# Twenty-four of the 368 expert-weight loads of a two-layer trunk, each split into three DMAs of 112, 8 and 8 partitions

## The reference

```python
def swiglu(h, w1, w3, w2):
    return (jax.nn.silu(h @ w1) * (h @ w3)) @ w2

def moe_swiglu(h, w_router, w1, w3, w2):
    logits = (xt @ w_router).astype(jnp.float32)
    top_val, top_idx = lax.top_k(logits, TOP_K)          # 2 of 8
    gate = jax.nn.softmax(top_val, axis=-1)
    ...
    for e in range(N_EXPERTS):
        y = y + combine[:, e:e + 1] * swiglu(xt, w1[e], w3[e], w2[e])
```

## Time and profile before

| | |
|---|---|
| median of three runs | 1189.1 us |
| profiled execution | 1189.25 us, its span 1187.3 us |
| PE busy | 1128.6 us, 95% of the span |
| DVE, ACT, POOL busy | 300.4, 200.4, 41.6 us |
| DMA | 418.11 MB, 352 GB/s over the span |
| first expert load issued | 239.8 us |
| last expert load issued, landed | 1147.2 us, 1173.95 us |

### The profile page before, as it was taken

One profiled execution on the slowest core, in us unless ns is written; L12 is line 12 of the kernel. 1 busy time (PEld: TensorE's weight loads), 2 busy tenths in 40 slices (PEclk: granted clock), 3 DMA queues, 4 the chain that ended last, 5 costly groups with the idle time before them and its releaser, 6 DMA issues.

```text
span 1187.3 us, 26595 instructions
## 1 busy us (share of the span) xinstructions
PE 1128.6 (95%) x12278; PEld 616.5 (52%) x12278; DVE 300.4 (25%) x408; ACT 200.4 (17%) x284; POOL 41.6 (4%) x37
## 2 busy tenths in 40 slices
PE   7999999999999999999999999977799999999775
PEld 6888888889763354353345335412333553354132
DVE  4654454459660111111110101111011111011002
ACT  5444434446631000000000000000000000000002
POOL 3000000001100000000000000000000000000000
PEclk9999999999999999999999999999999999999998
DMA  9975655553379999999999999999999999999994
GB/s 341 388 286 178 203 185 179 192 173 125 120 271 416 418 417 412 416 418 419 416 420 417 419 417 419 418 416 420 419 419 416 419 418 419 417 419 418 420 418 163
DMA packets 83528, 418.11 MB, mean 352 GB/s; under 512 B 8514, under 2 KB 14708, under 8 KB 69076
## 3 DMA queue, kind: packets, MB, share of 16 engines
q1 hardware_dynamic: 79952, 410.06, 86.6%
q0 software_dynamic: 1488, 4.59, 1.0%
q10 hardware_dynamic: 1972, 1.70, 0.4%
HBM read 414.23 MB, written 2.10 MB: 351 GB/s over the span
## 4 chain that ended last, share of the span: by engine, by line
PE 79%; DMA 12%; SPq 7%; issue 1%; ACT 1%; DVE 0%; ACTq 0%; DVEq 0%
PE psum L808 35%; PE psum L833 15%; DMA weights<-in_moe_w 11%; PE psum L716 8%; PE psum L718 8%; PE psum L717 8%; SPq L635 7%; DMA raw<-in_pool_w 1%; PE psum L916 1%; PE psum L795 1%; PE psum L785 1%; PE psum L724 0%; PE psum L1037 0%; PE psum L821 0%; PE psum L1014 0%
## 5 line engine op out<-in xcount | busy, mean ns | idle before, releaser
L808 PE MATMUL psum<-weights,xg 128*32 128x448 f32 x5328 | 513.0, 540 | 22.7 <-DMA weights<-in_moe_w 22.7
L808 PEld LDWEIGHTS psum<-weights,xg 128*32 128x32 f32 x5328 | 168.6, 110 | 358.6 <-issue 302.0
L833 PE MATMUL psum<-weights,hid_t 128*32 128x256 f32 x4704 | 260.9, 380 | 17.4 <-DMA weights<-in_moe_w 17.4
L833 PEld LDWEIGHTS psum<-weights,hid_t 128*32 128x32 f32 x4704 | 150.7, 110 | 129.1 <-DMA weights<-in_moe_w 26.4
L1490 DVE TENSOR_TENSOR low<-raw,high 128x2048 fp32r<-128x2048 f32 x50 | 114.6, 2291 | 85.5 <-ACT high L1199 85.3
L1610 DVE TENSOR_TENSOR sil<-sil,psum 128x1344 f32<-128x1344 f32 (+1 forms) x16 | 22.1, 1380 | 432.5 <-PE psum L808 432.5
L1199 ACT ACTIVATE high<-raw 128x2048 fp32r<-128x2048 f32 x51 | 97.8, 1918 | 82.6 <-PE psum L718 81.1
L716 PE MATMUL psum<-high,a_hi 128*128 128x512 f32 x224 | 87.3, 390 | 0.9 <-DVE a_lo L1527 0.9
L717 PE MATMUL psum<-high,a_lo 128*128 128x512 f32 x224 | 87.1, 389 | 0.0
L718 PE MATMUL psum<-low,a_hi 128*128 128x512 f32 x224 | 87.1, 389 | 0.0
L1263 ACT ACTIVATE sil<-psum 128x1344 f32<-128x1344 f32 (+1 forms) x16 | 18.4, 1151 | 389.2 <-PE psum L808 389.2
(11 more groups left out here) (241 smaller groups left out, 642.6 us busy)
## 6 DMA issues: line engine op xcount, KB each, us to landing
weights<-in_moe_w SPq DMA_DIRECT2D x256, 896.0 KB, 24.3
weights<-in_moe_w SPq DMA_DIRECT2D x112, 1024.0 KB, 26.0
raw<-in_ffn_w SPq DMA_DIRECT2D x42, 1024.0 KB, 7.2
raw<-in_w_q SPq DMA_DIRECT2D x4, 1024.0 KB, 5.1
raw<-in_w_o SPq DMA_DIRECT2D x4, 1024.0 KB, 5.1
x_res<-in_x SPq DMA_DIRECT2D x2, 512.0 KB, 5.3
raw<-in_pool_w SPq DMA_DIRECT2D x1, 1024.0 KB, 11.1
raw<-in_w_kv SPq DMA_DIRECT2D x1, 1024.0 KB, 5.4
```

The lines of the kernel that those rows point to most:

```text
L808: mm = pe.matmul(out3[g * BLK:(g + 1) * BLK, r, :], xg[:, k, r * BLK:(r + 1) * BLK], w[:, g], start=k == 0, stop=k == DT - 1)
L833: mm = pe.matmul(Y[g * BLK:(g + 1) * BLK, r, :], hid_t[:, c, r, b * BLK:(b + 1) * BLK], w[:, bb, g * GW:(g + 1) * GW], start=c == 0 and b ...
```

## The change

Units 10, 20 and 30 of each expert (all three of the 7168-byte kind) are issued as three DMAs: partitions 0 to 111, 112 to 119 and 120 to 127. A DMA over 112 partitions gives each of the 16 engines seven rows; one over eight partitions gives one row to each of eight engines. So eight of the engines carry 7 + 1 + 1 = 9 rows of such a unit and the other eight carry 7, where all sixteen carried 8. The bytes, their places and the order of the units stay. `landings(j)` counts how often the unit's semaphore is incremented in an expert up to unit j, 48 for a split unit and 16 for another, and `landed` builds PE's waits from it.

```diff
+UNEVEN = (10, 20, 30)
+EVEN_ROWS = 7 * P // 8
+
+
+def row_parts(j):
+
+    if j % MU in UNEVEN:
+        return slice(0, EVEN_ROWS), slice(EVEN_ROWS, EVEN_ROWS + 8), slice(EVEN_ROWS + 8, P)
+    return (slice(0, P),)
+
+
+def landings(j):
+
+    return 16 * sum(len(row_parts(i)) for i in range(j % NL, j + 1, NL))
@@ class Pass
             def landed(self, j, e):
-                return e * (16 * MU // NL) + 16 * (self.n0 * MU // NL + j // NL + 1)
+                return (e + self.n0) * landings(j % NL + MU - NL) + landings(j)
@@ expert_loads
                     sp.wait_ge(unit_used, ps.freed(j, e))
-                    sp.dma_start(expert_tile(ps, j, e), expert_source(who, *key)).then_inc(moe_landed[j % NL], 16)
+                    for rows in row_parts(j):
+                        sp.dma_start(expert_tile(ps, j, e)[rows],
+                                     expert_source(who, *key)[rows]).then_inc(moe_landed[j % NL], 16)
```

## The result

| | before | after |
|---|---|---|
| median of four runs (lowest to highest) | 1189.4 us | 1332.0 us (1327.7 to 1341.6) |
| profiled execution, its span | 1189.25, 1187.3 us | 1332.6, 1330.6 us |
| last expert load issued, landed | 1147.2, 1173.95 us | 1290.9, 1317.28 us |
| PE busy | 1128.6 us, 95% | 1163.4 us, 87% |

The ratio is 1.121, its 95% interval 1.115 to 1.127. The change makes the kernel 143 us slower. The forecast was 1220.7 us, with a range up to 1265: the direction was right, the size is four and a half times what was forecast (143 against 31.5 us), and it lies above the highest of my bounds, 1273 us.

What follows compares the result with a forecast made beforehand. The prediction took the 16 DMA engines as the bound: early engines' end 1159.3 + 6.6 for moved rows + 39.5 for small DMAs = 1205.4, plus 15.3 after the last landing = 1220.7 us; range 1184 to 1265.

Steps and rivals of the forecast that it cites:

- The bound: Whole stream: the 16 DMA engines never pause, at 416 to 420 GB/s; time is last landing plus 15.3 us.
- Rows moved: Split units: eight engines gain 6.6 us of rows, eight lose it; cost-free, last landing 2.1 us earlier, 1187.1 us.
- rival A: Small DMAs cost only their rows: 1187.1 us, or 1182.4 with the full balance; chance 0.30.
- SP: SP's issue of 48 more DMAs: 17 to 34 us, hidden behind 195 us of waits; nothing taken.
- Waits: PE's waits: once per unit as before, for a higher count; nothing added.
- The small DMAs themselves: Eight-row DMAs: three more row times, 0.82 us each, 39.5 us for 48; between nothing and 92 us.
- The sentence on the skill in the forecast: Skill's port rule: eight partitions reach two ports, 112 partitions break the one-to-one pattern; the sum would go above the forecast.
- The late half loses at most 19.7 us: Late engines where small rows come onto their partitions: 24 x 0.82 = 19.7 us, ending at 1193.4, not last.
- What would show it: Signs: share near 1, some 400 GB/s, PE's weight waits up by tens of us, last landing near 1205.
- B (the wrong half): Engines that get nine rows are the late ones, ending 6.6 us later: 1195.6 us; chance 0.08.
- C, 112 partitions on eight engines: The large DMA gives eight engines 14 rows, six more, 39 us: 1214 us; chance 0.10 together with D.
- D: SP becomes the pace, 48 small issues at 1.82 us make 87 us: some 1193 us; chance 0.10 together with C.

Runs made afterwards that it cites:

- experiment 12: Kernel before with unit 20 of every expert loading only its low 64 partitions, as eight DMAs of eight partitions four apart: 1190.9 us, ratio 1.0014.
- experiment 3: Changed kernel with the same 24 units as two DMAs of 64 partitions each instead of 112, 8 and 8: 1333.4 us, ratio 1.121.
- Experiment 1: Changed kernel with the same 24 units cut by columns into three DMAs, each over all 128 partitions: 1192.5 us, ratio 1.0027.
- experiments 2: Changed kernel with the same 24 units as two DMAs, of 112 and 16 partitions, none of eight rows: 1346.6 us, ratio 1.133.
- 14: Kernel before with unit 20 of every expert loading only its low 64 partitions, as eight DMAs of eight neighbouring partitions: 1215.4 us, ratio 1.0220.
- 13: Kernel before with unit 20 of every expert loading only its high 64 partitions, as eight DMAs of eight partitions four apart: 1219.8 us, ratio 1.0252.
- experiment 7: Changed kernel with its 112, 8 and 8 cut in unit 20 alone, eight units in all instead of 24: 1247.0 us, ratio 1.048.
- 8: Changed kernel with its 112, 8 and 8 cut in unit 20 alone and only in experts 0 to 3: 1211.2 us, ratio 1.0193.
- 9: Changed kernel with its 112, 8 and 8 cut in unit 20 alone and only in experts 4 to 7: 1216.5 us, ratio 1.0226.
- Experiment 15: Kernel before, all units uncut, 64 of 256 w1 and w3 units reading other memory rows, writes unchanged: 1189.2 us, ratio 1.000.

## Why the prediction was wrong

- *The bound*: right. The 16 DMA engines set the time; the whole loss is in their rate at a full share, and 13.3 us follow the last landing as before.
- *Rows moved*: right about the half that carries them (experiment 12). The halves do come level, but so they do in experiment 3, where no row moves, so the rows needn't be the reason. As in rival A, a few engines decide, and they trail by 16 us instead of 5.7. Whatever the balance gained can't be told beside 143 us.
- *SP* and *Waits*: right. Experiment 1 has all of both and costs 3 us; SP still waits 189 us for PE.
- *The small DMAs themselves*: **this step failed**, and twice. It put the price on the eight-row DMAs, 0.82 us each, 39.5 us in all; experiments 2 and 3 have none of them and are no faster, and eight-row DMAs alone cost 0.03, 0.41 and 0.48 us each in experiments 12, 14 and 13 (on other partitions than here). And it priced the 112-partition DMA beside them at nothing, so its upper end, eight rows one behind another in the small DMAs (1273), was no upper end. What the runs put in its place: the cut as a whole, whatever its parts (64 + 64 costs as much), slows all sixteen engines to about half, and more rows are slow than the cut units have (7760 more of 7168 bytes, for 3072). The account that fits experiments 12 to 14 is that a DMA over fewer partitions deals them out to the engines anew, so that engines write to partitions that another engine is writing to; it is argued from times, since no view names an engine. A cut unit costs 5.9 us, 22 row times of 0.274, where the forecast had 39.5/24 = 1.6. The sentence on the skill in the forecast said that the 112-partition DMA would break the one-to-one pattern; the sum didn't take it in, because no row of the kernel before showed a port shared. That missing row was a reason for a wide upper bound, not for none.
- *The late half loses at most 19.7 us*: wrong for the same reason; it was reckoned from 16 small rows a unit.
- *What would show it*: the signs were named rightly (share near 1, a falling rate, PE's waits growing by tens of us, landings late), the sizes not: 357 GB/s instead of some 400, 165 us more of waits on one line, the last landing at 1317 instead of 1205.
- *Rivals*: A (free) is out. B (the wrong half) is out by experiment 12. C, 112 partitions on eight engines, is out by the 384 additional packets. Its sum was wrong besides: with the two small rows these engines would carry 16, eight more than before, 53 us and not 39. D is out by SP's waits.

What stays open is the size. Counting rows that share a place gives less than measured (53 us expected for 64 + 64, 144 measured); 64 + 64 costs as much as 112 + 8 + 8; sixteen near and sixteen apart cost the same. That a dip grows with the lag of the halves is seen in experiment 7 and only partly borne out by 8 and 9. No run has the 112-partition DMA without others beside it. Experiment 15 excludes one other pattern of reading, not every one.

## What to carry to other kernels

In a stream that keeps all sixteen DMA engines busy, a DMA over all 128 partitions is one case and a cut by partitions another: one in fifteen units cut so cost 12%, and the price falls on the uncut neighbours too. The one cut that cost next to nothing, experiment 12, loads half a unit in a pattern that fits the uncut one. If a load must be split, split it by columns (0.3% here). And a price sheet for a split has to hold every part of it, the large remainder first, since that is where most of the bytes are.

## What the runs showed of the hardware

- At a DMA share of 1.0 the rate can be half: 222 GB/s against 418 to 430 a few us later, on all sixteen engines together. The share tells whether the engines are occupied, the GB/s whether they get on; only the two together show this loss. Between 822 and 826 us every row took 422 ns or more, where 274 is usual.
- DMAs over eight partitions, four apart, in the low half: 1.8 us for 64 of them. From the high half: 31 us. The same low half in neighbours: 26 us.
- Three DMAs in place of one, over the same 128 partitions: 3 us for 48 more, 0.07 us each.
- A DMA over eight partitions adds eight completion packets and one over 112 adds sixteen (384 more for 24 cut units).
- With the halves level, two or three engines alone ended 16 us after the others.
